# A streaming encoder step on one core: attention outputs in three slots stored by SyncE, alternating score banks, the first input matrices built in the last head, and value products split around the gate matmuls

## What is computed

```python
h = rmsnorm(x, norm_mix_g);  z = h @ w_in
u_pool, u_ssm, q, k, v, logf, gates = columns of z      # gates: sigmoid, 3 x 1024 columns
y_a = pool_mixer(u_pool, ...)                           # trailing-window means
y_b, state = ssm_mixer(u_ssm, ...)                      # 32 groups of 16 channels, 64 complex states each
c = cumsum(logf)                                        # per head
for each of 8 heads:                                    # fox_attention
    s = q @ k.T * scale + c_q - c_k                     # causal mask per frame
    y_c = softmax(s) @ v
x = x + (sum_n gates[n] * (y_n @ w_branch[n])) @ w_out
x = x + ((silu(conv_g(up)) * conv_v(up)) @ w_down),  up = rmsnorm(x) @ w_up
y = rmsnorm(x)
```

## Time and profile before

| | us |
|---|---|
| median of 3 runs | 1920.14 |
| lowest, highest | 1918.97, 1920.38 |
| the profiled execution | 1920.72 |
| its span, first to last instruction | 1919.0 |

### The profile page before, as it was taken

One profiled execution on the slowest core, in us unless ns is written; L12 is line 12 of the kernel. 1 busy time (PEld: TensorE's weight loads), 2 busy tenths in 40 slices (PEclk: granted clock), 3 DMA queues, 4 the chain that ended last, 5 costly groups with the idle time before them and its releaser, 6 DMA issues. The chain is left out here.

```text
span 1919.0 us, 28813 instructions
## 1 busy us (share of the span) xinstructions
PE 1859.6 (97%) x11323; PEld 1803.0 (94%) x11323; DVE 1186.5 (62%) x1820; ACT 432.2 (23%) x812; POOL 808.8 (42%) x461
## 2 busy tenths in 40 slices
PE   7999999989997999999999999999999999999997
PEld 6989999888987989989999999999999999999997
DVE  6688653888874456444573587556556556556556
ACT  4210123555551111140011221111111111111113
POOL 4434344333327456322232355535535535525530
PEclk8999999999998999999999999999999999999999
DMA  8634839664725544256541111111111111111102
GB/s 269 177 129 131 259 117 259 169 169 129 183 70 156 122 94 110 72 173 220 184 172 45 45 55 56 44 33 55 44 33 55 44 33 55 44 33 55 44 23 95
DMA packets 221949, 203.97 MB, mean 106 GB/s; under 512 B 58305, under 2 KB 200621, under 8 KB 221154
## 3 DMA queue, kind: packets, MB, share of 16 engines
q1 hardware_dynamic: 199250, 166.00, 30.3%
q10 hardware_dynamic: 22608, 36.72, 5.7%
HBM read 138.44 MB, written 59.77 MB: 103 GB/s over the span
## 5 line engine op out<-in xcount | busy, mean ns | idle before, releaser
L154 PE MATMUL bank<-act_hi,w_hi 128*128 128x364 f32 (+1 forms) x2544 | 848.1, 333 | 9.4 <-DVE act_lo L1454 3.8
L154 PE MATMUL bank<-act_lo,w_hi 128*128 128x364 f32 (+1 forms) x2544 | 837.7, 329 | 0.0
L154 PE MATMUL bank<-act_hi,w_lo 128*128 128x364 f32 (+1 forms) x2544 | 836.9, 329 | 0.0
L154 PEld LDWEIGHTS bank<-act_hi,w_hi 128*128 128x128 f32 x2544 | 479.6, 189 | 16.6 <-issue 10.8
L154 PEld LDWEIGHTS bank<-act_lo,w_hi 128*128 128x128 f32 x2544 | 479.3, 188 | 1.0 <-issue 0.3
L154 PEld LDWEIGHTS bank<-act_hi,w_lo 128*128 128x128 f32 x2544 | 479.0, 188 | 0.0
L2731 DVE SCALAR_TENSOR_TENSOR conv<-up_raw,cw,conv 128x1090 f32<-128x1090 f32 x86 | 179.9, 2092 | 63.8 <-ACT up_raw L2617 33.5
L2414 POOL CAST w_hi<-w_raw 128x1024 fp32r<-128x1024 f32 x44 | 47.5, 1080 | 356.8 <-PE bank L154 351.7
L154 PE MATMUL bank<-ffn_hi,down_hi 128*128 128x364 f32 (+1 forms) x528 | 174.0, 330 | 0.7 <-DVE up_raw L2765 0.5
L154 PE MATMUL bank<-ffn_lo,down_hi 128*128 128x364 f32 (+1 forms) x528 | 173.0, 328 | 0.0
L154 PE MATMUL bank<-ffn_hi,down_lo 128*128 128x364 f32 (+1 forms) x528 | 172.7, 327 | 0.0
(11 more groups left out here) (302 smaller groups left out, 2461.4 us busy)
## 6 DMA issues: line engine op xcount, KB each, us to landing
w_raw<-in_w_up SPq DMA_DIRECT2D x44, 512.0 KB, 3.8
w_raw<-in_w_in SPq DMA_DIRECT2D x42, 512.0 KB, 4.5
gate<-gate_scratch ACTq DMA_DIRECT2D x24, 544.0 KB, 4.1
w_raw<-in_w_down SPq DMA_DIRECT2D x22, 512.0 KB, 3.3
gate_scratch<-gate_out ACTq DMA_DIRECT2D x48, 182.0 KB, 2.4
w_raw<-in_w_branch SPq DMA_DIRECT2D x12, 512.0 KB, 4.0
kh<-kh_scratch SPq DMA_DIRECT2D x16, 336.0 KB, 7.5
kl<-kl_scratch SPq DMA_DIRECT2D x16, 336.0 KB, 8.5
```

The lines of the kernel that those rows point to most:

```text
L154: mm = pe.matmul(out, w(k), x(k)[:, c0:c0 + cn], start=first and k == ks[0] and n == 0, stop=last and k == ks[-1] and n == 2)
```

## The change

The edit has six parts, all of them around the attention and the start of the mixer.

1. `o_hi` and `o_lo` become three slots (256, 256 and 64 columns): groups 0 to 3 of a head alternate between the first two, the fifth (the 64 sample frames) has the third. Each slot has its own semaphore.
2. `out_store` moves from ACT to SP, whose stream becomes a loop over the units: at its place in each iteration it stores an output, loads the next head, or loads a gate block. The q, k and `nck` loads of a head stay on the event that frees their buffers; the values' and the gate blocks' loads have places of their own.
3. Units with 512 keys or fewer (x = 4 to 8) use bank 1 and bank 2 in turn; `score` of x = 5 to 8 waits only for `row_max(n - 2)`.
4. `pv` is called twice: all high products but the last before the gate half, the low products and the last high one after it.
5. `qs`, `kh`, `kl`, `nck` become separate buffers for even and odd heads, placed so that the even ones' space can be taken, during the last head (an odd one), by the first tile's `tab` and input matrices. POOL does the six steps of `inputs(0)` one by one in iterations x = 1 to 6 of the last head (`input_step`, new); the table is loaded at the place where the head after would be.
6. After the barrier POOL splits gate blocks 12 and 13 one after the other, and goes on with `inputs(1)`; SP no longer loads `tab` of tile 0 and gate block 13 there.

```diff
-        oh, ol = sb("o_hi", [HD, 2, 256], F32R), sb("o_lo", [HD, 2, 256], F32R)
+        oh, ol = sb("o_hi", [HD, 512 + TS], F32R), sb("o_lo", [HD, 512 + TS], F32R)
...
             banks = (nk + 511) // 512
-            return banks, nk // banks
+            return banks, nk // banks, 0 if banks == 2 else n % UNITS % 2
+
+        def scores_read(n):
+            return n if n % UNITS < 5 else n - 1
+
+        def out_slot(g):
+            h, i = divmod(g, 5)
+            return (i % 2, 256 * (i % 2), 2 * h + i // 2) if i < 4 else (2, 512, h)
...
+            for n in range(N + 3):
+                h, i = divmod(n + 2, UNITS)
+                if i == 0 and 1 <= h <= HEADS - 1:
+                    sp.wait_ge(score_done, UNITS * h)
+                    sp.wait_ge(top_done, UNITS * h)
+                    if h < HEADS - 1:
+                        load_qk(sp, h + 1)
+                        load_terms(sp, h + 1)
+                    else:
+                        sp.dma_start(m.tab[0][:], m.tab_d[:, 0:NB]).then_inc(m.tab_ld[0], 16)
+                if n - 1 in group_of:
+                    out_store(group_of[n - 1])
+                h, i = divmod(n - 2, UNITS)
+                if i == 0 and 1 <= h < HEADS - 1:
+                    sp.wait_ge(pv_done, 5 * h)
+                    load_values(sp, h + 1)
+                if n - 2 in free_at:
+                    load_gate(free_at[n - 2] + 2)
...
+                step = n - (N - UNITS) - 1
+                if 0 <= step < 6:
+                    input_step(pool, m, 0, *divmod(step, 3))
...
                 if n:
-                    pe.wait_ge(top_done, n)
+                    pe.wait_ge(top_done, scores_read(n))
...
                 if n in group_of:
-                    pv(group_of[n])
+                    pv(group_of[n], False)
                 if n in half_of:
                     gate_piece(*half_of[n])
-                elif n in piece_of:
+                elif n in piece_of and n < N:
+                    gate_piece(piece_of[n])
+                if n in group_of:
+                    pv(group_of[n], True)
+                if n >= N:
                     gate_piece(piece_of[n])
...
+                a, c0, count = out_slot(g)
                 act.wait_ge(o_sum_done, g + 1)
-                act.wait_ge(o_st[g % 2], 32 * (g // 2) + 32)
+                act.wait_ge(o_st[a], 32 * count + 32)
...
-                if n - 1 in group_of and n - 1 < N and n != N:
-                    out_store(group_of[n - 1])
...
+def input_step(pool, m, t, h, part):
+    g, did = slice(4 * h, 4 * h + 4), m.pool_did
+    powers = lambda c: m.tab[t % 2][:, g, c:c + C].unsqueeze(3).to_broadcast([P, 4, C, SC])
+    matrix = lambda c: m.tab[t % 2][:, g, c:c + SC].unsqueeze(2).to_broadcast([P, 4, C, SC])
+    if part == 0:
...
+        pool.tensor_tensor(m.w[:, g], powers(PR), matrix(B1), ALU.mult).then_inc(*did.mark(f"w_a{h}{t}"))
+    elif part == 1:
+        pool.tensor_tensor(m.wt[:], powers(PI), matrix(B2), ALU.mult).then_inc(*did.mark(f"w_b{h}{t}"))
+    else:
+        pool.wait_ge(*did.at(f"w_b{h}{t}"))
+        pool.tensor_tensor(m.w[:, g], m.w[:, g], m.wt[:], ALU.add).then_inc(*did.mark(f"w{t}" if h else f"w0_{t}"))
...
-        load_tab(0)
-        load_gate(GATE0 + 2)
         load_tab(1)
...
         gate_split(12)
-        inputs(0)
         gate_split(13)
         inputs(1)
```

More of the change, by code:

```diff
@@ L713, in high @@
                                      stop=b == len(blocks) - 1)
-                for b in range(len(blocks) - 1):
-                    high(b)
+                if not late:
+                    for b in range(len(blocks) - 1):
+                        high(b)
+                    return
                 pe.wait_ge(p_lo, n + 1)
@@ L744, in scalar @@
         def scalar(act):
-            for a in range(2):
+            for a in range(3):
                 act.sem_inc(o_st[a], 32)
@@ L1757, in mix_engines @@
     tiles = range(MW)
-    tab_ld, ut_ld = [sem(f"tab_ld{a}") for a in range(2)], [sem(f"ut_ld{t}") for t in tiles]
+    tab, w, tab_ld, ut_ld = m.tab, m.w, m.tab_ld, [sem(f"ut_ld{t}") for t in tiles]
     u2_ld = [sem(f"u2_ld{a}") for a in range(2)]
```

173 lines of the change are left out of this document (87 added, 86 removed).

## The result

| | before | changed |
|---|---|---|
| median, us | 1920.26 (4 runs, 1918.97 to 1921.80) | 1902.54 (4 runs, 1898.91 to 1904.29) |
| ratio | 1 | 0.9903, 95% interval 0.989 to 0.9916 |
| the profiled execution, us | 1920.72 | 1903.40 |
| its span, us | 1919.0 | 1901.6 |

The kernel is 17.7 us faster; 24.5 had been forecast (1895.6). Why 7 us are missing is the subject of what follows, since the changed kernel turned out to leave 14 us more to be had in the attention.

The account below looks back on a forecast made before the run. PE, busy for 97% of the span, was taken as the bound, its waits as the gain: 11.6 + 8.5 + 3.1 + 3.8 - 1.0 - 1.5 = 24.5 us, so 1895.6 us, range 1888.5 to 1907.

Parts of the forecast that it names:

- The mixer's start: First transposes after the barrier: PE's wait for POOL's input matrices and the clock drop behind it go, 11.6 us gained.
- Stores and slots: Attention, head boundaries: ACT's out_high no longer waits for stores, so PE's waits for prob_high go, 8.5 us gained.
- The split: Attention: value product around the gate half hides PE's waits for prob_low, except at x = 5; 3.1 us gained.
- (b): Attention: the value product's later end delays out_part, exp, out_sum and row_max, costing 1.5 us over 24 covered groups.
- rival 1: Attention: late value product makes a round trip PE waits for in every covered group, 10 us, about 1904; chance 0.16.
- The banks: Attention scores in two banks: four waits for row maxima go and half of four others, 3.8 us gained.
- (a): Last head: POOL's six input steps, four falling on an out_low of DVE, cost 1.0 us.
- Rival 2: Last head: POOL's steps reach PE in full, 6.8 us instead of 1.0, plus a late mask, about 1902; chance 0.06.
- (c): SP's new places: it waits behind o_lo with only loads for the head after queued behind; no cost given.
- Rival 4: Head boundaries: stores queue behind a head's loads and ACT waits, 36 us of PE, 1940, slower than before; chance 0.04.

Follow-up runs that it names:

- plain: Changed kernel with value product in one part, scores in one bank, SP's old opening load order, input steps held until the last unit is normalised: 1891.70 us, 0.9851.
- one_bank: Changed kernel with every unit's scores starting in bank 1 again, each waiting for the row maxima of the unit before: 1902.00 us, 0.9902.
- late_inputs: Changed kernel with POOL's six input steps back behind the barrier, between the splits of gate blocks 12 and 13: 1904.28 us, 0.9907.
- act_store: Changed kernel with output stores issued by ACT again at their old places, three slots kept: 1907.03 us, 0.9932.
- gate3_first: Changed kernel with SP's opening loads in their old order, gate block 3 ahead of head 1's q, k and nck: 1901.54 us, 0.9892.

## Why the prediction was right, and where it was wrong

- **The mixer's start, -11.6.** Right in mechanism and size: 9.0 in E and 2.3 in F. Nothing else came up late; `cl` and gate block 13 were in time, as worked out.
- **Stores and slots, -8.5.** Right in mechanism, too small in size. The whole gain of stretch B, 13.8 us, goes to these two parts: with either of them undone B is 182.1 or 182.8, with banks and split undone (plain) it is still 176.3. The "3.8" of the banks was booked on the wrong account: seven of the eight waits for row maxima came from ACT being late, by the two DMAs it issued and by its waits for slots, which I had said of four and then taken only half. The eighth, 0.30 us at 325.42 us, is the one behind gate block 2; I had counted it among those four. What the rows of waits show of stretch B (12.1 us in 10 gaps before, 3.1 in 6 after, 0.2 us more for each gap, and 1.7 of clock) is 11.5 us; the other 2.3 show in no wait, and stay open.
- **The split, -3.1 and (b) +1.5.** The waits at x = 0 went, as said, and those at x = 5 stayed. What failed is the size of (b) and its mechanism: I had the chain right as far as `out_sum`, and then followed it to `row_max` and the next `turn` (rival 1). What PE waited for was `gate_scale`, which also stands behind `out_sum` on DVE: 1.9 us in 4 gaps in stretch B, each before the next iteration's gate half. Taken together the split is worth nothing in B and costs about 1 us in A. Rival 1's round trip of 0.4 us per group did not appear.
- **The banks, -3.8.** Worth nothing that shows (one_bank, plain).
- **(a) POOL's steps in the last head, +1.0.** This is the step that failed most: 7.6 us. Rival 2 (6.8, given a chance of 0.06) had the size, but only part of the route: of the four `out_low` of the head two were stretched, to 1.96 and 2.15 us. Three things were wrong in my term. I took the average of before, where a third of DVE's lost time reached PE, for places where little stood between DVE and PE. I counted `out_low` only, with its two SBUF inputs; `normalise`, which has one and stands directly ahead of PE's transposes, took 2.04, 1.58 and 1.32 us instead of 0.65, 0.35 and 0.29 (the second beside the `low` step of gate block 11, which an input step had pushed there). And I had no term for the clock, 3.1 us behind these gaps, though I had one for the gaps of before.
- **Not seen at all: the loads at the start.** In (c) I passed SP's new order as free. In its opening, head 1's loads now come 0.5 us behind gate block 2 instead of 2.8, and PE's wait behind that block grew from 0.3 to between 1.15 and 2.6 us; 3.6 us in the profiled execution, about 1 by the medians, which is within their noise. That these loads delay the block is argued from the order alone; no run varied the bytes.
- **Rival 4, the stores behind a head's loads.** Did not occur: no store was waited for. With two slots, stores on the same queue, ACT waits 8.5 us for them: it is the third slot that gave the time.

The account of the profiled executions: 24.5 forecast; 0.3 less at the mixer; 6.1 less in C and D (7.1 lost where 1.0 was allowed); 3.6 less in A; B as forecast in sum (13.8 against 8.5 + 3.1 + 3.8 - 1.5 = 13.9, though part of these terms belongs to other stretches). That gives 14.4. The remaining 3.0 of the 17.4 us lie in the stretches that the change does not touch, 1.8 before the attention and 1.2 after the second tile; the attention begins at 309.8 to 311.8 us in the thirteen profiles, so I take these 3 us as no part of the change.

That B came out as summed is luck: banks and split were worth nothing there, and slots and stores gave as much more. The mixer's start, and that ACT's waits for slots would go, were understood; that the total lies in the range is owed to its width, since it came out at the price of rival 2, to which I had given 0.06.

## What to carry to other kernels

Work that is moved onto an idle engine is not free if it shares something with the engine that is waited for. Look for a stretch in which the *neighbour* has nothing urgent, and hold the moved work back to it with a wait; here one wait turned 8 us of loss into none. Before splitting or reordering the consumer's work to hide a late step, try to take the cause of the lateness out of that step's way: swapping two DVE instructions, with the value product in one part, gained 3.4 us in stretch B, where the split that was meant to hide them gained none. And where two edits aim at one wait, undo each alone, since a sum of waits does not tell which cause makes them all.

## What the runs showed of the hardware

- A DVE step with a single SBUF input is stretched by a POOL step as one with two inputs is: `normalise` of 128 x 384 took 2.04 us beside a POOL step of 1.93 and 0.65 us without. The Trainium skill ("SBUF — State Buffer", section "SBUF: two separate sides") is cited in the prediction for two SBUF inputs; the same sentence of it also names VectorE instructions in a 2-port perf mode. Whether `normalise` runs in such a mode no row here shows, but it is stretched the same way. `prob_low`, with one input in PSUM, took 0.54 us for 128 x 384 right beside POOL's step at 559.83, and 0.56 in before without one.
- PE's clock answered gaps of not very different length, at the same place of the program, in two ways: it was 1.00 in the windows at and after a wait of 1.62 us (late_inputs), 0.99 and then 0.58 at and after one of 1.84 (act_store). In the last head three gaps of 1.0 to 1.75 us in eight were followed by 0.50.
- SP was held 6.44 us by the issue of a single DMA of 16 KB, the sixteenth that it issued within 9 us; the same one held it for 4.41 us in the kernel before and 4.12 in gate3_first. A full queue would explain it, but no row shows that. In the order of the change gate block 3 is behind it, and was issued at 333.23 us:

```profile
321.54 6.44 SPq L588 DMA_DIRECT2D vhl<-vh_scratch  x1
...
333.23 1.14 SPq L596 DMA_DIRECT2D w_raw<-in_w_in  x2
```
